# Coefficient tiles of the down products placed at four other remainders by 512 bytes

## The reference, cut to what matters

```
# block 1: D_FF = 8192
u = relu(h2 @ w_up);            x = x + (u * u) @ w_down
# block 2: 16384 experts, gates are zero but for 16 of them in each of 8 heads
hid = gelu(x . u_e);            y = sum over experts of (gate * hid) * v_e
```

## Time and profile before

| | us |
|---|---|
| median of 3 runs | 3318.03 |
| lowest and highest | 3316.56, 3321.89 |
| span of the profiled execution, first to last instruction | 3316.7 |
| its TensorE busy time | 3251.2 |

### The profile page before, as it was taken

One profiled execution on the slowest core, in us unless ns is written; L12 is line 12 of the kernel. 1 busy time (PEld: TensorE's weight loads), 2 busy tenths in 40 slices (PEclk: granted clock), 3 DMA queues, 4 the chain that ended last, 5 costly groups with the idle time before them and its releaser, 6 DMA issues.

```text
span 3316.7 us, 48331 instructions
## 1 busy us (share of the span) xinstructions
PE 3251.2 (98%) x20054; PEld 2896.3 (87%) x20054; DVE 2039.7 (61%) x1849; ACT 1459.5 (44%) x1268; POOL 486.7 (15%) x418
## 2 busy tenths in 40 slices
PE   7999999999999989999999999999999999999998
PEld 6788899999999878888879999999999888888886
DVE  4455565555555557665456888999874555455554
ACT  5564453344333464453334444455543333333333
POOL 0000000000000002135200002888840000000000
PEclk9999999999999999999999999999999999999999
DMA  6444465555555443342245565676676666556563
GB/s 255 141 164 165 154 229 191 191 191 194 193 193 190 141 164 127 130 150 89 90 164 217 194 223 216 213 247 234 230 252 239 231 236 251 221 224 253 231 237 114
DMA packets 131396, 644.18 MB, mean 194 GB/s; under 512 B 14640, under 2 KB 47664, under 8 KB 61872
## 3 DMA queue, kind: packets, MB, share of 16 engines
q1 hardware_dynamic: 96016, 624.18, 52.4%
q10 hardware_dynamic: 35232, 17.83, 1.8%
HBM read 606.31 MB, written 35.66 MB: 194 GB/s over the span
## 4 chain that ended last, share of the span: by engine, by line
PE 92%; DVE 3%; ACT 2%; DMA 1%; issue 1%; SPq 0%; DVEq 0%; ACTq 0%
PE pj L288 12%; PE pj L289 12%; PE pj L287 12%; PE pj L275 7%; PE pj L274 7%; PE pj L273 7%; PE pj L1637 3%; PE pj L1639 3%; PE pj L1638 3%; PE pj L818 3%; PE pj L820 3%; PE pj L819 3%; PE pm L273 2%; PE pt L273 2%; PE pt L274 2%; PE pm L275 2%
## 5 line engine op out<-in xcount | busy, mean ns | idle before, releaser
L255 ACT ACTIVATE hi<-raw 128x2048 fp32r<-128x2048 f32 x535 | 1025.0, 1916 | 1419.2 <-PE pj L289 661.5
L262 DVE TENSOR_TENSOR lo<-raw,hi 128x2048 fp32r<-128x2048 f32 x400 | 917.1, 2293 | 714.3 <-ACT hi L255 713.7
L287 PE MATMUL pj<-xh,hi 128*128 128x256 f32 x3328 | 927.0, 279 | 0.0
L289 PE MATMUL pj<-xh,lo 128*128 128x256 f32 x3328 | 926.1, 278 | 0.0
L288 PE MATMUL pj<-xl,hi 128*128 128x256 f32 x3328 | 926.0, 278 | 0.0
L287 PEld LDWEIGHTS pj<-xh,hi 128*128 128x128 f32 x3328 | 630.8, 190 | 0.6
L288 PEld LDWEIGHTS pj<-xl,hi 128*128 128x128 f32 x3328 | 625.0, 188 | 0.6
L289 PEld LDWEIGHTS pj<-xh,lo 128*128 128x128 f32 x3328 | 624.8, 188 | 0.0
L262 DVE TENSOR_TENSOR lo_in<-raw,hi 128x2048 fp32r<-128x2048 f32 x135 | 311.4, 2310 | 281.3 <-ACT hi L255 280.7
L2314 POOL TENSOR_SCALAR hotA<-cst,slotT 128x128 fp32r<-128x128 f32 x256 | 328.2, 1297 | 496.2 <-ACT slotT L2157 435.8
L1637 PE MATMUL pj<-hi,xh 128*128 128x512 f32 x576 | 235.7, 409 | 13.4 <-ACT proj L1706 7.3
(11 more groups left out here) (382 smaller groups left out, 4269.8 us busy)
## 6 DMA issues: line engine op xcount, KB each, us to landing
raw<-w_peer SPq DMA_DIRECT2D x256, 1024.0 KB, 6.1
raw<-w_mlp SPq DMA_DIRECT2D x128, 1024.0 KB, 4.9
raw<-w_in SPq DMA_DIRECT2D x104, 1024.0 KB, 4.9
raw<-w_out SPq DMA_DIRECT2D x32, 1024.0 KB, 4.8
raw<-w_q SPq DMA_DIRECT2D x16, 1024.0 KB, 5.0
act_scratch<-hidU SPq DMA_DIRECT2D x32, 512.0 KB, 3.1
gates_scratch<-stage ACTq DMA_DIRECT2D x8, 2048.0 KB, 16.9
hidV<-act_scratch SPq DMA_DIRECT2D x32, 512.0 KB, 3.7
```

What stands on the lines that cost most here:

```text
L255: nc.scalar.activation(hi[:, j, :], raw[:, j, :], ACT.Copy).then_inc(hi_ready, 1)
L262: nc.vector.tensor_tensor(low(q)[:, j, :], raw[:, j, :], hi[:, j, :].bitcast(F32), ALU.subtract).then_inc(lo_ready, 1)
L287: nc.tensor.matmul(o, hi[:, j, cols], xh[:, k0 + k, :], start=clears, stop=False, skip_group_check=True)
L289: mm = nc.tensor.matmul(o, lo[:, j, cols], xh[:, k0 + k, :], start=False, stop=end and b % 2 == 1, skip_group_check=True)
```

## The change

`place`, which lays a tile behind the one before, gets an argument `rest`: it first moves the cursor up to the next offset with that remainder by 512. The eight coefficient tiles use it. Counted from `at_raw`: `coef_h0` and `coef_l0` go to remainder 0, `coef_h1` and `coef_l1` to 256, `cV_h0` and `cV_l0` to 64, `cV_h1` and `cV_l1` to 128. The weights stay at 0. Nothing else is edited: not an instruction, a wait or a transfer.

```diff
-            def place(name, shape, dt=F32):
+            def place(name, shape, dt=F32, rest=None):
+
+                if rest is not None:
+                    c[0] += (rest - c[0]) % 512
                 t = sb(name, shape, dt, at=c[0])
                 c[0] += (4 * int(np.prod(shape[1:])) + 31) // 32 * 32
@@
-        coef_h = [y(f"coef_h{i}", [P, 4, TT * P], F32R) for i in range(2)]
-        coef_l = [y(f"coef_l{i}", [P, 4, TT * P], F32R) for i in range(2)]
+        coef_h = [y(f"coef_h{i}", [P, 4, TT * P], F32R, rest=(at_raw + 256 * i) % 512) for i in range(2)]
+        coef_l = [y(f"coef_l{i}", [P, 4, TT * P], F32R, rest=(at_raw + 256 * i) % 512) for i in range(2)]
         rs_wide = y("rs_wide", [P, TT, P])
         rs_row = y("rs_row", [P, TT * P])
@@
-        cV_h = [y(f"cV_h{i}", [P, 4, TT * P], F32R) for i in range(2)]
-        cV_l = [y(f"cV_l{i}", [P, 4, TT * P], F32R) for i in range(2)]
+        cV_h = [y(f"cV_h{i}", [P, 4, TT * P], F32R, rest=(at_raw + 64 + 64 * i) % 512) for i in range(2)]
+        cV_l = [y(f"cV_l{i}", [P, 4, TT * P], F32R, rest=(at_raw + 64 + 64 * i) % 512) for i in range(2)]
         last_sq = y("last_sq", [P, TT, D])
```

## The result

| | before | changed |
|---|---|---|
| median, us | 3319.32 (20 runs) | 3323.89 (20 runs) |
| lowest and highest | 3316.39, 3323.64 | 3322.26, 3328.27 |
| span of the profiled execution | 3316.7 | 3326.2 |

The ratio is 1.0014, with a 95% interval of 1.0008 to 1.0021. The median is 3.9 us over the 3320 that was predicted and inside its range. The time moved little, but not because little happened: two effects of opposite sign, both larger than the one that was forecast, cancel in part.

The account below looks back on a forecast made before the run. The prediction took TensorE, which waits for nobody, to bound the kernel. 3316.7 plus 2.1 us (block 1's distance-0 down products, other terms zero) gave 3318.8 for the profiled span, 3320 on the median; range 3305 to 3340.

Parts of the forecast that it names:

- the same: Whole kernel: a time of 3311.4 to 3324.7 us, about 0.2% (6.6 us) from no change; chance 0.52.
- the two rhythms: TensorE's matmul pitches: short (113 and 229 ns) or long (117.6 and 233.3), about 4.4 ns a matmul apart.
- Block 1, distance 0 at +2.7 ns from the decay sums: Block 1's down products, half at distance 0: 768 x 2.7 ns = +2.1 us, the middle of +1.1 to +4.4 ns.
- Distance 256 at nothing: The other half of block 1's 1536 down products, at distance 256: no cost, 0.
- Distance matters in the long rhythm only: TensorE's products: distance changes the pitch by a few nanoseconds in the long rhythm, not in the short one.
- Removed, added, moved: zero: All queues: no instruction, wait or transfer changes; paddings shift rs_wide, rs_row and last_sq, serving few small operations; zero.
- V stretch at 0: V stretch, 3072 products at distances 64 and 128 in the long rhythm: 0 us, between bounds +13.5 and -56 us.
- Rival A: Block 1 tips into the long rhythm: 18.6 us on up and down products, about 3339; chance 0.15.
- Rival B: V stretch: new distances dearer in the long rhythm, +2 to +4.4 ns, +6 to +13.5 us, 3326 to 3333; chance 0.17.
- Rival C: V stretch falls into the short rhythm: 3072 x -4.4 = -13.5 us, 3306.6; chance 0.12.
- Rival D: V stretch: one of its distances reaches 215 ns a product; chance 0.08.
- Rival E: Whole kernel: the distance acts in neither rhythm, 3318; chance 0.10.

Follow-up runs that it names:

- e2: The kernel before with rs_wide and rs_row behind it moved to remainder 256, coefficients still at 192; 3325.5 us, ratio 1.0012.
- e7: e4 with block 1's coefficients at 64 (even) and 128 (odd), the V stretch's at 64, rs_wide at 192; 3311.6 us.
- e1: The changed kernel with rs_wide put back at remainder 192; 3329.5 us, ratio 1.0024.
- e6: The kernel before with block 1's coefficients all at 256, the V stretch's all at 0, rs_wide at 192; 3313.7 us.
- e4: The kernel before with hotA moved to remainder 0, 48 KB further on, and hotG with the tile behind it 4096 bytes forward; 3285.3 us, ratio 0.9894.
- e5: e4 with the V stretch's coefficients at 0 (even blocks) and 256 (odd blocks); 3278.7 us, ratio 0.9874 to the kernel before.
- e8: e4 with xh, xl and all regions behind them, coefficients included, moved from remainder 192 to 256; 3337.2 us, ratio 1.0052.
- e9: e4 with xh and all behind it at 64, block 1's coefficients and rs_wide at 192, the V stretch's coefficients at 0; 3312.6 us.
- e10: e4 with xh and all behind it at 128, block 1's coefficients and rs_wide at 192, the V stretch's coefficients at 0; 3345.1 us.
- e11: e4 with block 1's coefficients all at 448, the V stretch's all at 384, rs_wide at 192; 3296.0 us.

## Why the prediction was right, and where not

The forecast, "the same", and its range held. Its mechanism did not: the likeliest case was +2.1 us made of one small term, and what came was +11.5, +0.6, -3.4 and -1.6 (with the V stretch's), about +7 in the touched stages. So the number held by luck: 12 us of up products that the sum did not have, against 7 us by which the down products of both stretches came out cheaper than in it, and a median that lies 0.8 us inside the upper edge of "the same".

- **What bounds the kernel, the two rhythms, and that the distance acts through them**: right. Nothing on ACT or DVE mattered (each pair's waits in the V stretch are the same to 2.5 us), and the pitches are the whole story.
- **Block 1, distance 0 at +2.7 ns from the decay sums**: wrong in sign. It was the nearest row in kind, but three products between others say little: e2 and e7 show that a pitch depends on what ran before, so rows of a stream's middle were wanted, and none had distance 0. Measured: -2.2 ns.
- **Distance 256 at nothing**: wrong, -2.2 ns. That it would be like 0 could have been asked: the tail products made me take 512 bytes for the period, since their durations at distance 0 and 256 differ, 282 against 277 ns. In those rows, durations with loads of 8 to 16 columns, they do; in the pitches with loads of 128 columns the runs show no difference.
- **"Distance matters in the long rhythm only"**: wrong. At 0 and 256 the pitch is 226.7 in either, at 64 it is 233.3 in either.
- **Removed, added, moved: zero**: wrong by 0.6 us. The shifted `rs_wide` tipped up(1) (e1, e2). Four matmuls were thought too few to count; what they cost is not their own time.
- **V stretch at 0, the tail rows of distance other than 0 being within 2 ns of each other**: right in size (-1.6 us, inside the bounds), but the reason does not carry over to 512 columns: there distances other than 0 differ by 6.6 ns (226.7 at 256 in e6, 233.3 at 64 in e7). The sign named for being wrong, over 4 ns for one of the four distances, did not come in the changed kernel: its down products moved by 2.2 ns in block 1 and by 1.0 at most in the V stretch.
- **Rival A (0.15)**: its mechanism happened, and this is what the likeliest case lacked: it had the up products at no cost. Up products behind the down quads went to 117.8 and stayed: 11.5 us of the 11.8 it gave them. Its other half, down products at +4.4 ns, came out at -2.2 ns, which is why the total stayed inside "the same". Its reason, that the gate products tip the rhythm by their distance, is borne out by e4, with the reservation made there. Distance 0 is not the whole of it: 256 tips the up products too (e6), 64 as well (e7), and the transposes ahead of up(0) end the long rhythm at distance 0.
- **Rival B**: V did not get dearer. **Rival C**: V in the short rhythm is real and worth 13.7 us, but at distance 192 and with e4's edit. Distance 0 gives 20.4 us without that edit (e6).
- **Rival D (0.08), one of the V stretch's distances at 215 ns, and the lower bounds of both stretches**: they rest on the earlier trace rows, (88.36 - 87.93) / 2 = 215 ns for a pass of 256 float32 columns. That a down product could come near it was the author's estimate, and no run shows one that does: the lowest pitch of a stretch with 512 columns is 226.7 (e5, e6, e8).
- **Rival E, the distance acts in neither rhythm**: the runs disagree. Moving tiles, with no instruction changed, moves the pitch from 226.7 to 233.3 ns (e6, e7). That the load of the next stationary operand and the read of the moving one, which overlap in time, hinder each other is no more than a guess: it is not shown, since no run had one without the other.

Open: what a rhythm is. The runs show that it is kept from product to product, which distances hold or leave it, and what it costs; not what state of TensorE or of its reads it is. Two states are too few: e9's down products are short between long up products. Open too is why 512 columns are cheapest where 256 columns are dearest, and why an up quad (with `xh` at 192) is short behind down products at 128, 192 and 448 and long behind 0, 64 and 256.

## What to carry to other kernels

Where TensorE is the bound with fp32r operands, take the pitch (start to start) of the same line in every stage; if it differs at the same clock, look at the operands' offsets by 256 bytes first. A few small matmuls with another distance can set the pitch of thousands behind them (256 had set that of some 7200, e4), so move operands one tile at a time, check every tile behind a padding, and read each stage's time, not the total. Distances worth trying first: 0 for products of 512 columns with nothing narrower behind them (e5), and 64 for all products of 256 columns that run in turn (e4). Equal distances alone are not enough: at 0 and at 128 they gave the two slowest versions (e8, e10).

## What had not been expected of the hardware

- The same matmul, with the same shape, clock and operands' addresses, has two lasting pitches: 113.3 and 117.8 ns with 256 columns, 228.9 and 233.3 with 512. Which one is entered depends on the products before (e2, e4).
- Sixty-four groups of four gate products at distance 0 cost the kernel before 35 us, 1% of its time, nearly all of it in other products (e4).
- The dependence repeats every 256 bytes where it was tried (e6, e11), and distance 0 is the cheapest with 512 moving columns and among the dearest with 256 (e8).
- Where the steps of a stream are even, they are 113.3 or 120.0 ns with 256 columns and 226.7 or 233.3 with 512: 6.7 ns apart each time. The values between are means of uneven steps (225 to 232 ns for the 228.9 of block 1 before).
